# A two-layer encoder step: the first projection is computed from x without its reciprocal norm, and GpSimd multiplies the norm into each tile that it stores

## The chip, the cores and the metric

The kernel runs on one core of a Trainium2 chip. The metric is the device time of one execution, in microseconds (us). The three runs before the change took 2880.22, 2878.37 and 2882.38 us, with a median of 2880.22. A matmul runs on TensorE (PE in the profile; PEld is its weight load). DVE is VectorE, ACT is ScalarE, POOL is GpSimd, and SP is the queue that issues most transfers.

## The reference

Two layers work on 544 tokens (512 of a prompt and 32 of a second sequence) with 1024 channels. What matters here is the start of each layer:

```python
h = x * rsqrt(mean(x * x) + 1e-6) * g          # _rmsnorm, one factor per token, one gain per channel
a_q, a_k, a_v, a_f, b_q, b_k, b_v, c_in, gate_in = split(h @ w_in)   # 7944 columns wide
log_f = log_sigmoid(a_f + fox_forget_bias)
...                                            # three mixers: FoX attention, differential attention, RWKV-7
gates = sigmoid(gate_in)                       # 3 x 1024
y = sum(gates * proj) @ w_out
x = x + rmsnorm(y); x = x + rmsnorm(cross_attention(...)); x = x + rmsnorm(swiglu(...))
```

The reciprocal norm of a token is one number for all channels of that token. So it can be multiplied into the result of the projection instead of into its input: `(x * r * g) @ w = r * ((x * g) @ w)`.

## The kernel before

Everything is kept transposed: a tile has 128 channels as partitions and the 544 tokens as columns, so x is 8 such tiles (`xT`). A matmul takes 272 tokens (`HT`). To reach float32 accuracy with the fast matmul format, each operand is split into a high and a low part, and three products are summed (high x high, high x low, low x high): a tile of 128 output channels over 1024 input channels is 8 x 3 x 2 = 48 matmuls. Weights come in units of 128 output columns through a ring of 4 buffers that SP fills (`unit`, L447). DVE splits each unit into `WHI` and `WLO` (`split_unit`, L1867), of which there are two buffers; a unit's split starts when the tile that used that buffer is done.

The engines run five programs, written out by hand, that wait for each other by semaphores. Three barriers per layer (`phase_end`, L414) join PE, ACT, DVE and POOL; SP waits for the second one.

The start of a layer, before the change:
- layer 0 only: PE transposes the eight tiles of x (`setup`, L646, into three pairs of banks), ACT and DVE copy the two halves out.
- PE transposes the gain vectors (L777), ACT copies them to `VT`. ACT squares the 8 tiles of x (L1430); PE sums each over the channels (`norm_sums`, L692); ACT makes the reciprocal norm `RS` by Ln and Exp (`norm_rstd`, L1399).
- DVE splits weight units 0 and 1 (L1890, L1891). At the change of layers it does so after it has updated x (`postnorm`, L1849: hT * gain * RS, then xT += hT).
- After the first barrier, DVE makes h = x * gain * RS, its high and its low part, two tiles at a time (`prenorm_split`, L1834), and PE computes the tiles of units 0 and 1 together as the pairs arrive (`dense_first`, L748). From unit 2 on `dense_split` (L726) computes one tile after the other, all from the same `HH` and `hTR`.

The projection's results: 12 full tiles (`EST`, 4 buffers) and the forget gate's 8 rows in the first part; 26 tiles as 52 halves in fill between the attention's steps (`late`, `ESTL`, 4 buffers of a half); 24 gate tiles, of which 22 go out as 44 halves (`GST`), and the last two stay in the chip (`GS`, L1693: ACT applies the sigmoid as it copies them from PSUM). ACT (and DVE) copy a result from PSUM, POOL issues the store to DRAM, and SP loads it again where it is used. POOL computes nothing.

In front of the FFN the kernel already works in another manner: DVE updates x tile by tile, ACT makes the high part of x * gain as soon as a tile is updated, DVE the low part (`updated` and `low`, L2362 to L2370), `dense_first` starts with the first of them, the sums of squares are taken between its matmuls (`group_sums`, L673, and `sums_spread`, L685), and the reciprocal norm is multiplied in by DVE when it reads the results.

Of the kernel before, what the change touches and what calls it, by code (L numbers as in the profile page):

```python
# [8 lines left out]
F32 = mybir.dt.float32  # L9
# [3 lines left out]
ALU = mybir.AluOpType  # L13
# [41 lines left out]
X_SPLITS = 4 + 6 + 8  # L55
# [106 lines left out]
def build_program(nc, A, C_const, C_rope, O):  # L162
# [7 lines left out]
    with ExitStack() as ctx:  # L170
        def sb(name, shape, dt=F32):
            return ctx.enter_context(nc.sbuf_tensor(name, shape, dt))
# [7 lines left out]
        def sem(name):  # L180
            return ctx.enter_context(nc.semaphore(name))
# [16 lines left out]
        lam4 = sb("lam4", [P, 4, HEAD_DIM])  # L198
        lamp = sb("lamp", [P, 2, HEAD_DIM])
# [75 lines left out]
        FST = cv(3, 4)  # L275
        ESTL = carver(NU - KM * T - 4 * HT)(4, HT)
# [5 lines left out]
        for h in range(2):  # L282
# [65 lines left out]
        SUM_OF = (0, 6, 0, 6, 6, 6)  # L348
        SUMS_AT = (1, 2, 4, 5, 7, 8)
# [6 lines left out]
        ident_loaded, consts_loaded, x_loaded, x_put_act, setup_pe, consts_ready = (  # L356
            sem(n) for n in ("ident_loaded", "consts_loaded", "x_loaded", "x_put_act", "setup_pe", "consts_ready"))
# [283 lines left out]
        def _(pe):  # L641
# [3 lines left out]

            def setup():  # L646

                for a in range(KM):
                    if a % 4 == 0:
                        pe.wait_ge(*((x_loaded, 32) if a == 0 else (far_half, 16)))  # L650
                    if a >= 3:
                        pe.wait_ge(x_put_act, a - 2)
                        pe.wait_ge(x_updated, a - 2)
                    q = 2 + 2 * (a % 3)
                    for b in range(4):
# [29 lines left out]
            def sums_spread(l, k):  # L685

                pe.wait_ge(sums_put, l * 2 + k // 2)
# [85 lines left out]
            for l in range(DEPTH):  # L773

                pe.wait_ge(vec_loaded, (l + 1) * 16 * 19)
                pe.wait_ge(tile_freed_act, l * TILES + 4)
                tr(PS[:, 4, 0:NVEC], VR[0:NVEC, :], ident[0:NVEC, 0:NVEC]).then_inc(vec_turned, 1)  # L777
                norm_sums(l, 0)

                phase_end(pe, l, 0)  # L780
# [4 lines left out]
                dense_first(l, G_IN, 0, of_h_split, 0)  # L785
                for v in range(2, N_IN):
                    dense_split(l, G_IN + v, IN_PAIR[v], v, of_h_split, exact=(v == FORGET_AT), rot=IN_ROT[v])
# [442 lines left out]
                for n in range(N_BR):  # L1230
                    if n == 3:
                        pe.wait_ge(gt_evac, l * 48 + 50)
                    dense_split(l, G_BR + n, n % 4, V_BR + n, of_branch(n % 3), need=4 + 2 * n if n < 3 else None)
# [105 lines left out]
                dense_first(l, G_FFI, V_FFI, of_f, 10, sums=4)  # L1339
# [31 lines left out]
        def _(act):  # L1371
# [27 lines left out]
            def norm_rstd(l, k, to=RS):  # L1399

                if k in (2, 4):
                    act.wait_ge(sums_done, l * 8 + SUMS_AT[k] - 1)
# [3 lines left out]
                act.wait_ge(sums_done, l * 8 + SUMS_AT[k])  # L1406
                for h in range(2):
                    f(half(RS, h), PS[:, SUM_OF[k] + h, 0:HT], ACT.Ln, scale=1.0 / (D_MODEL * (GROUP if k in (2, 4) else 1)), bias=eps[:, 0:1])
# [15 lines left out]
            for l in range(DEPTH):  # L1424

                act.wait_ge(vec_turned, l + 1)
                copy(VT[:, 0:NVEC], PS[:, 4, 0:NVEC])
# [368 lines left out]
        def _(dve):  # L1796
# [12 lines left out]
            for a in range(KM):  # L1809
                dve.wait_ge(setup_pe, a + 1)  # L1810
                copy(xT[:, a, 2 * P:T], PS[:, 3 + 2 * (a % 3), 0:T - 2 * P]).then_inc(x_updated, 1)
            dve.wait_ge(ident_loaded, 16)
            dve.wait_ge(consts_loaded, 16)
            copy(identb[:, :], const("ident"))
            copy(mfoxb[:, :], const("mfox"))
            copy(mdiffb[:, :], const("mdiff"))
            dve.drain().then_inc(consts_ready, 1)

# [66 lines left out]

            for l in range(DEPTH):
# [3 lines left out]
                split_unit(l, 0)  # L1890
                split_unit(l, 1)  # L1891
                phase_end(dve, l, 0)
                prenorm_split(l, 0, "norm_mix_pre", HH)
# [3 lines left out]
                for v, j in enumerate(IN_ORDER):  # L1897
                    tile(l, G_IN + v)
                    split_unit(l, v + 2)
                    if j is None:  # L1900
                        for h in range(2):
                            ts(half(TZ[0:8, 0, :], h), PS[0:8, 6 + h, 0:HT], small[0:8, 20:21], None, ALU.add)
# [523 lines left out]
                postnorm(l, 5, "norm_ffn_post")  # L2426
# [9 lines left out]
        def _(pool):  # L2436
# [10 lines left out]
            for l in range(DEPTH):  # L2447

                for name, row in _v.items():
# [10 lines left out]
                    allow_slow_non_contiguous=True).then_inc(vec_loaded, 16)  # L2460
                dma(lam4[:, :, :].rearrange("p a b -> p (a b)"),
                    A["diff_lambda"][ds(l, 1)].rearrange("l a b -> l (a b)").to_broadcast([P, 256])) \
                    .then_inc(vec_loaded, 16)
                dma(PLF[:, :, :], A["cache_fox_logf"][ds(l, 1)].rearrange("l b (t p) h -> p (l b t) h", p=P)) \
                    .then_inc(plf_loaded, 16)
                wait(vec_loaded, (l + 1) * 16 * 19)
                wait(plf_loaded, (l + 1) * 16)
                phase_end(pool, l, 0)


# [5 lines left out]
                for v, j in enumerate(IN_ORDER):  # L2476
# [3 lines left out]
                    wait(tile_freed_dve, l * TILES + G_IN + v + 5)  # L2480
                    dma(proj_d[j * P:(j + 1) * P, :], EST[:, e % 4, :]).then_inc(est_stored[e % 4], 16)
# [19 lines left out]
                def late_store(q):  # L2501

                    wait(late_evac, l * 2 * N_LATE + q + 2)
                    r, h = (12 + LATE_ORDER[q // 2]) * P, q % 2
                    dma(proj_d[r:r + P, h * HT:(h + 1) * HT], ESTL[:, q % 4, :]).then_inc(late_stored[q % 4], 16)
                    if q >= 2:
                        late_kept(q - 2)
# [55 lines left out]
                def gate_store(q, it=0):  # L2563

                    for h in range(2):
                        wait(gt_evac, l * 48 + 2 * q + h + 3 + it * 16)
                        r = GATE_ORDER[q + it * 8] * P
                        dma(gate_d[r:r + P, h * HT:(h + 1) * HT], GST[:, q % 2, h, :]) \
# [39 lines left out]
                gate_kept(21)  # L2608
                wait(shift_stored, (l + 1) * 32)
# [5 lines left out]
                wait(sums_done, l * 8 + 2)  # L2615
# [51 lines left out]
```

## Time and profile before

| | |
|---|---|
| median of 3 runs | 2880.22 us |
| the profiled execution | 2874.14 us, span 2872.3 us |
| PE busy | 96% of the span |
| DVE / ACT / POOL busy | 56% / 26% / 9% |
| mean granted TensorE clock | 0.991 |

Busy means that an instruction of that engine ran. A line of a timeline gives start, duration, engine, line of the kernel, the operation, output and input, and, where the engine had been idle, for how long and who released it.

### The profile page before, as it was taken

How to read it: one execution, taken by the hardware profiler on the slowest of the kernel's cores; microseconds unless marked ns; L12 is line 12 of the kernel's file. 1: busy time of each engine (PE TensorE's matmuls, PEld its weight loads, DVE VectorE, ACT ScalarE, POOL GpSimd, SP SyncE). 2: the span in 40 equal slices, each digit the busy share in tenths (PEclk: the TensorE clock that was granted, in tenths of full speed). 3: DMA queues.
4: the chain of work that ended last, by engine and by line, in shares of the span. 5: the costliest groups of instructions: out<-in, count | busy, mean ns of one | idle time of the engine just before them, and what ended most of it. 6: DMA issues, size and time to landing. Idle time of an engine off the chain costs nothing.

```text
span 2872.3 us, 63037 instructions
## 1 busy us (share of the span) xinstructions
PE 2750.8 (96%) x26472; PEld 2571.1 (90%) x26472; DVE 1611.0 (56%) x2967; ACT 753.7 (26%) x1803; POOL 244.2 (9%) x423
## 2 busy tenths in 40 slices
PE   7999999999999989999989999999999998999998
PEld 6877889999999789999988778899999996999997
DVE  5444665666664266664374455556666533766633
ACT  1143343333332330000112433433223324200001
POOL 1221112000000100000001211110000000000000
PEclk9999999999999999999999999999999999999999
DMA  4453436222263133333234434452224532233231
GB/s 136 127 144 105 144 107 170 72 72 65 82 173 100 46 89 89 89 87 88 77 90 132 120 111 139 103 160 72 72 68 115 153 92 73 71 89 89 85 88 58
DMA packets 420762, 290.26 MB, mean 101 GB/s; under 512 B 38544, under 2 KB 386352, under 8 KB 420352
## 3 DMA queue, kind: packets, MB, share of 16 engines
q1 hardware_dynamic: 398496, 228.64, 28.7%
q0 software_dynamic: 21984, 57.59, 6.3%
q8 instruction: 210, 3.44, 0.5%
q14 instruction: 72, 0.59, 0.1%
HBM read 232.12 MB, written 54.07 MB: 100 GB/s over the span
## 4 chain that ended last, share of the span: by engine, by line
PE 80%; DVE 8%; ACT 3%; DVEq 3%; DMA 2%; issue 2%; ACTq 0%; SPq 0%
PE PS L744 35%; PE PS L813 10%; PE PS L1116 8%; PE PS L1049 7%; PE PS L722 4%; PE PS L1258 2%; DMA U<-gate_scratch 2%; ACT U L1373 1%; PE PS L859 1%; PE PS L1090 1%; ACT U L1376 1%; PE PS L895 1%; PE PS L763 1%; PE PS L974 1%; PE PS L1194 1%
## 5 line engine op out<-in xcount | busy, mean ns | idle before, releaser
L744 PE MATMUL PS<-U_r,WHI 128*128 128x272 f32 x2656 | 474.4, 289 | 12.5 <-DVEq L2285 9.0
L1376 ACT COPY U<-PS 128x272 f32<-128x272 f32 (+9 forms) x782 | 273.1, 373 | 728.3 <-PE PS L1116 139.8
L1865 DVE CAST WHI<-ring 128x1024 fp32r<-128x1024 f32 (+1 forms) x240 | 164.1, 684 | 473.3 <-PE PS L744 365.3
L744 PEld LDWEIGHTS PS<-U_r,WHI 128*128 128x128 f32 x2656 | 386.1, 188 | 18.1 <-DVEq L2285 13.2
L744 PE MATMUL PS<-brT_r,WHI 128*128 128x272 f32 x1728 | 357.3, 288 | 1.4 <-DVEq L1876 1.4
L744 PE MATMUL PS<-U_r,WLO 128*128 128x272 f32 x1696 | 350.0, 288 | 0.0
L744 PE MATMUL PS<-hT_r,WHI 128*128 128x272 f32 x1696 | 349.7, 288 | 0.0
L1875 DVE TENSOR_TENSOR WLO<-ring,WHI 128x1024 fp32r<-128x1024 f32 (+1 forms) x240 | 289.7, 1207 | 19.4 <-issue 1.3
L744 PE MATMUL PS<-brT_r,WLO 128*128 128x272 f32 x1344 | 278.2, 288 | 0.0
L744 PEld LDWEIGHTS PS<-brT_r,WHI 128*128 128x128 f32 x1728 | 271.5, 188 | 2.2 <-DVEq L1876 2.2
L813 PE MATMUL PS<-U_r,WHI 128*128 128x272 f32 x832 | 261.6, 314 | 12.2 <-ACT U L1376 12.0
L744 PEld LDWEIGHTS PS<-hT_r,WHI 128*128 128x128 f32 x1696 | 266.5, 189 | 0.0
L744 PEld LDWEIGHTS PS<-U_r,WLO 128*128 128x128 f32 x1696 | 265.6, 188 | 0.0
L813 PE MATMUL PS<-U_r,WLO 128*128 128x272 f32 x832 | 242.1, 291 | 0.0
L813 PE MATMUL PS<-hT_r,WHI 128*128 128x272 f32 x832 | 241.0, 290 | 0.0
L1049 PE MATMUL PS<-U_r,WHI 128*128 128x272 f32 x768 | 229.7, 299 | 2.8 <-DVEq L2080 2.4
L1049 PE MATMUL PS<-U_r,WLO 128*128 128x272 f32 x768 | 221.8, 289 | 0.0
L1049 PE MATMUL PS<-hT_r,WHI 128*128 128x272 f32 x768 | 220.9, 288 | 0.0
L1116 PE MATMUL PS<-U 64*64 64x64 f32 (+1 forms) x5184 | 213.2, 238 | 0.0
L744 PEld LDWEIGHTS PS<-brT_r,WLO 128*128 128x128 f32 x1344 | 209.8, 189 | 0.0
L1116 PEld LDWEIGHTS PS<-U 64*64 64x64 f32 x5184 | 207.2, 134 | 1.3
L813 PEld LDWEIGHTS PS<-U_r,WHI 128*128 128x128 f32 x832 | 158.7, 191 | 31.5 <-issue 15.0
(336 smaller groups left out, 4291.5 us busy)
## 6 DMA issues: line engine op xcount, KB each, us to landing
ring<-in_w_in_dram SPq DMA_DIRECT2D x126, 512.0 KB, 4.3
ring<-in_w_ffn_in_dram SPq DMA_DIRECT2D x88, 512.0 KB, 3.8
ring<-in_w_ffn_out_dram SPq DMA_DIRECT2D x32, 448.0 KB, 3.7
proj_scratch<-U POOLq DMA_DIRECT2D x104, 136.0 KB, 2.1
U<-proj_scratch SPq DMA_DIRECT2D x48, 272.0 KB, 4.2
ring<-in_w_branch_dram SPq DMA_DIRECT2D x48, 256.0 KB, 3.2
gate_scratch<-U POOLq DMA_DIRECT2D x88, 136.0 KB, 3.2
U<-gate_scratch SPq DMA_DIRECT2D x44, 272.0 KB, 2.9
```

Of the source, the lines that this page charges most:

```text
L722: ins = mm(PS[0:width, 2 * q + h, 0:HT], ring[:, n % RING, k, 0:width], rhs(k, h), start=(k == 0), stop=(k == kn - 1))
L744: ins = mm(PS[:, 2 * q + h, 0:HT], w, half(x, h), start=(first and k == 0 and n == 0), stop=(last and k == kn - 1 and n == len(terms) - 1))
L763: ins = mm(PS[:, 2 * j + h, 0:HT], w, half(x, h), start=(k == 0 and n == 0), stop=(k == KM - 1 and n == 2))
L813: ins = mm(PS[:, 7, 0:HT], w, half(x, h), start=(k == 0 and i == 0), stop=(k == 7 and i == 2))
L859: mm(PS[:, b, 0:n], q, FK[it % 2][0:66, h, 0:n], start=True, stop=False)
L895: ins = mm(PS[o, 6, i * P:(i + 1) * P], FVT[it % 2][:, h, t, :], pt[:, t * P:(t + 1) * P], start=(t == 0), stop=(t == i))
L1049: ins = mm(PS[:, 6 + h, 0:HT], w, half(x, h), start=(k == 0 and i == 0), stop=(k == 7 and i == 2))
L1116: ins = mm(PS[r, bank, cols], w_c[r], x_c[r], start=(n == 0), stop=(n == len(pairs) - 1))
L1258: ins = mm(PS[:, 2 + n % 4, u * P:(u + 1) * P], MNT[:, k, t * P:(t + 1) * P], ring[:, (U_MEM + 2 * s + u) % RING, k, :], start=(k == 0), s ...
L1376: return act.copy(out, in_)
L1865: copy(hi, src)
L1875: tt(lo, w, hi.bitcast(F32), ALU.subtract)
```

## The change

- **Projection input.** `HH` becomes the high part of x * gain, written by ACT (`high`), and `hTR` its low part, by DVE (`low_in`), one tile at a time, without the reciprocal norm. `dense_first` waits per tile (8 signals where there were 4) and has the sums of squares between its matmuls, in banks 4 and 5. The reciprocal norm goes to a buffer of its own, `RSI`, which lives until the gates.
- **Results.** POOL multiplies each tile or half by `RSI` before it issues the store (`scaled`): per layer 12 tiles, 52 late halves and 44 gate halves. The two gate tiles that stay in the chip are copied raw, multiplied by POOL, and then go through ACT's sigmoid in place. DVE multiplies the forget gate's 8 rows.
- **Order at the start.** In layer 0 DVE splits units 0 and 1 between its copies of x (after tiles 4 and 6), and PE transposes the vectors ahead of tile 6. At the change of layers DVE splits them as soon as the FFN's last tile is done, and then updates x and makes the low parts in one sequence (`update_and_split`).
- `diff_lambda` is loaded after the first barrier, into another place, and the first barrier is signalled but no longer waited for by PE, ACT and DVE.

The diff, cut to its core:

```diff
-                pe.wait_ge(vec_loaded, (l + 1) * 16 * 19)
-                pe.wait_ge(tile_freed_act, l * TILES + 4)
-                tr(PS[:, 4, 0:NVEC], VR[0:NVEC, :], ident[0:NVEC, 0:NVEC]).then_inc(vec_turned, 1)
-                norm_sums(l, 0)
-                phase_end(pe, l, 0)
+                if l > 0:
+                    pe.wait_ge(tile_freed_act, l * TILES + 4)
+                    vectors(l, 4)
+                pe.drain().then_inc(bar, 1)
-                dense_first(l, G_IN, 0, of_h_split, 0)
+                dense_first(l, G_IN, 0, of_h_split, 0, sums=0)
+                sums_spread(l, 0)
...
+                def high(a):
+                    act.wait_ge(x_updated, l * 24 + a + 1)
+                    f(HH[:, a, :], xT[:, a, :], ACT.Copy, scale=vec("norm_mix_pre", a)).then_inc(h_ready, 1)
-                for a in range(KM):
+                for a in range(0, KM, 2):
+                    high(a)
+                    high(a + 1)
                     norm_square(l, 0, a)
-                norm_rstd(l, 0)
-                phase_end(act, l, 0)
+                    norm_square(l, 0, a + 1)
+                norm_rstd(l, 0, RSI[:, :])
...
                 for q in (22, 23):
                     for h in range(2):
                         act.wait_ge(gt_done, l * 48 + 2 * q + h + 1)
-                        f(half(GS[:, q - 22, :], h), PS[:, 6 + h, 0:HT], ACT.Sigmoid).then_inc(gt_evac, 1)
+                        copy(half(GS[:, q - 22, :], h), PS[:, 6 + h, 0:HT]).then_inc(gt_evac, 1)
+                    gate_cast(q + 2)
+                for q in (22, 23):
+                    act.wait_ge(gs_scaled, l * 2 + q - 21)
+                    f(GS[:, q - 22, :], GS[:, q - 22, :], ACT.Sigmoid)
                     act.drain().then_inc(gs_ready, 1)
-                    gate_cast(q + 2)
                 phase_end(act, l, 1)
...
+            def low_in(l, b):
+                dve.wait_ge(h_ready, l * 24 + b + 1)
+                stt(hTR[:, b, :], xT[:, b, :], vec("norm_mix_pre", b), HH[:, b, :].bitcast(F32), ALU.mult, ALU.subtract) \
+                    .then_inc(x_split, 1)
+            def update_and_split(l):
+                dve.wait_ge(rstd_ready, l * 6 + 6)
+                scale(0); scale(1); dve.drain(); add(0); add(1)      # scale: hT * gain * RS; add: xT += hT
+                for b in range(2, KM, 2):
+                    scale(b); scale(b + 1); dve.drain()
+                    low_in(l + 1, b - 2); low_in(l + 1, b - 1)
+                    add(b); add(b + 1)
+                low_in(l + 1, KM - 2); low_in(l + 1, KM - 1)
+            for a in range(KM):
+                dve.wait_ge(setup_pe, a + 1)
+                copy(xT[:, a, 2 * P:T], PS[:, 3 + 2 * (a % 3), 0:T - 2 * P]).then_inc(x_updated, 1)
+                if a == 4:
+                    split_unit(0, 0)
+                if a == 6:
+                    split_unit(0, 1)
...
-                postnorm(l, 5, "norm_ffn_post")
+                if l == DEPTH - 1:
+                    postnorm(l, 5, "norm_ffn_post")
+                else:
+                    tile(l, G_FFO + N_FFO - 1)
+                    split_unit(l + 1, 0)
+                    split_unit(l + 1, 1)
+                    dve.drain().then_inc(bar, 1)
+                    update_and_split(l)
...
+                def scaled(t, h=None):                                # POOL
+                    by = RSI[:, :] if h is None else half(RSI, h)
+                    pool.tensor_tensor(t, t, by, ALU.mult)
+                    pool.drain()
+                    scaled(EST[:, e % 4, :])                          # ahead of the store, and so for ESTL and GST
                     dma(proj_d[j * P:(j + 1) * P, :], EST[:, e % 4, :]).then_inc(est_stored[e % 4], 16)
```

## Rows read from the trace of the kernel before

**Rows 1.** The page: busy time, share of the span and instructions of each engine.
```profile
PE 2750.8 (96%) x26472; PEld 2571.1 (90%) x26472; DVE 1611.0 (56%) x2967; ACT 753.7 (26%) x1803; POOL 244.2 (9%) x423
```
**Rows 2.** The chain that ended last, its longest pieces: start us, us, what.
```profile
34.79 13.20 PE PS L763 x84
50.49 14.31 PE PS L744 x112
...
1043.88 385.41 PE PS L744 x3072
1468.35 14.29 PE PS L744 x112
```
**Rows 3.** Timeline at the change of layers.
```profile
1429.12 2.91 PE L703 MATMUL PS<-brT,ones 128*128 128x272 f32 x12
...
1433.72 1.48 DVE L1858 SCALAR_TENSOR_TENSOR hT<-hT,small,U 128x544 f32<-128x544 f32 x2 [13.15 <-ACTq L1411]
```
**Rows 4.** Timeline of the start of the FFN in layer 0.
```profile
1034.83 1.12 PE L680 MATMUL PS<-U,ones 128*32 128x272 f32 x16
...
1041.80 0.69 DVE L1865 CAST WHI<-ring 128x1024 fp32r<-128x1024 f32 x1 [3.04 <-PE PS L763]
```
**Rows 5.** Timeline of the first 30 us.
```profile
10.99 0.52 POOL L2459 DMA_DIRECT2D small<-in_fox_forget_bias_dram  x1
...
14.22 0.46 DVE L1811 COPY xT<-PS 128x288 f32<-128x288 f32 x1 [0.83 <-PE PS L657]
...
15.40 1.11 PE L656 MATMUL PS<-CB,U 128*128 128x128 f32 x4
...
19.49 0.69 DVE L1865 CAST WHI<-ring 128x1024 fp32r<-128x1024 f32 x1
...
21.60 0.69 DVE L1865 CAST WHI<-ring 128x1024 fp32r<-128x1024 f32 x1
```
**Rows 6.** Transfers issued at 3.3 to 3.9 and 4.4 to 12 us: KB, us to landing.
```profile
ring<-in_w_in_dram SPq DMA_DIRECT2D x1, 512.0 KB, 11.8
...
small<-in_fox_forget_bias_dram POOLq DMA_DIRECT2D x1, 0.0 KB, 5.1
```
**Rows 7.** Groups of instructions: shapes, count | busy us, mean ns | idle before.
```profile
L2369 DVE SCALAR_TENSOR_TENSOR hT_r<-xT,VT,brT_r 128x544 fp32r<-128x544 f32 x16 | 12.5, 779 | 0.2
...
L1855 DVE TENSOR_TENSOR xT<-xT,hT 128x544 f32<-128x544 f32 x32 | 21.8, 722 | 1.2
...
L1373 ACT ACTIVATE brT_r<-xT,VT 128x544 fp32r<-128x544 f32 x16 | 12.0, 749 | 17.0 <-DVE xT L2365 17.0
```
**Rows 8.** Stretches: length, busy us of PE, PEld, DVE, ACT, POOL, granted clock, DMA.
```profile
29.30:33.00 3.70, 0.00 (x0) 0.00 (x0) 1.94 (x3) 1.47 (x3) 0.00 (x0) 1.00 0.00 0
34.79:40.00 5.21, 5.21 (x23) 5.21 (x24) 4.95 (x7) 0.00 (x0) 0.00 (x0) 0.50 0.01 3
```
**Rows 9.** Timeline from the last gate tile into the branch projection, layer 0.
```profile
759.47 0.62 ACT L1376 CAST WHI<-ring 128x512 fp32r<-128x512 f32 x1
...
760.14 0.69 DVE L2103 TENSOR_TENSOR WLO<-ring,WHI 128x512 fp32r<-128x512 f32 x1 [1.14 <-ACTq L1581]
...
766.78 0.52 PE L744 MATMUL PS<-U_r,WHI 128*128 128x272 f32 x2 [1.23 <-DVEq L2285]
```
**Rows 10.** Timeline of ACT among the first gate tiles.
```profile
475.26 0.39 ACT L1376 COPY U<-PS 128x272 f32<-128x272 f32 x1 [2.70 <-POOLq L2561]
```
**Rows 11.** POOL's groups of instructions: count | busy us, mean ns | idle before.
```profile
L2505 POOL DMA_DIRECT2D proj_scratch<-U x104 | 57.3, 551 | 451.3 <-ACT U L1376 400.8 <-DVEq L2080 41.9 <-issue 8.6
L2568 POOL DMA_DIRECT2D gate_scratch<-U x88 | 48.1, 548 | 206.1 <-ACT U L1376 200.0 <-issue 6.2
```
**Rows 12.** Timeline of the preparation of one RWKV recurrence.
```profile
550.28 0.87 ACT L1376 COPY U<-PS 128x272 f32<-128x272 f32 x2
...
550.38 1.36 DVE L2134 TENSOR_TENSOR U<-U 128x545 f32<-128x545 f32 x2
...
554.44 1.24 PE L1090 MATMUL PS<-U,CB 128*128 128x288 f32 x4 [0.40 <-DVE U L2157]
```

More of the change, by code:

```diff
@@ L54 @@
 SPLITS = V_FFO + 8 * len(FFO_SPLIT)
-X_SPLITS = 4 + 6 + 8
+X_SPLITS = 8 + 6 + 8
 def unit_of(v):
@@ L644, in _, with vectors @@
             pe.wait_ge(ident_loaded, 16)
+            def vectors(l, bank):
+                pe.wait_ge(vec_loaded, l * 16 * 19 + 16 * 18)
+                tr(PS[:, bank, 0:NVEC], VR[0:NVEC, :], ident[0:NVEC, 0:NVEC]).then_inc(vec_turned, 1)
             def setup():
@@ L654, in setup @@
                     q = 2 + 2 * (a % 3)
+                    if a == 6:
+                        vectors(0, 0)
                     for b in range(4):
@@ L1337, in of_f @@
                     return HF[:, k, :], hTR[:, k, :]
-                dense_first(l, G_FFI, V_FFI, of_f, 10, sums=4)
+                dense_first(l, G_FFI, V_FFI, of_f, 14, sums=4)
                 sums_spread(l, 4)
@@ L1405, in norm_rstd @@
                     act.drain().then_inc(sums_put, 1)
-                act.wait_ge(sums_done, l * 8 + SUMS_AT[k])
+                act.wait_ge(sums_done, l * SUMS + SUMS_AT[k])
                 for h in range(2):
-                    f(half(RS, h), PS[:, SUM_OF[k] + h, 0:HT], ACT.Ln, scale=1.0 / (D_MODEL * (GROUP if k in (2, 4) else 1)), bias=eps[:, 0:1])
+                    f(half(RS, h), PS[:, SUM_OF[k] + h, 0:HT], ACT.Ln, scale=1.0 / (D_MODEL * (GROUP if k in (0, 2, 4) else 1)), bias=eps[:, 0:1])
                 act.drain()
@@ L1808, in _ @@
             dve.sem_inc(df_evac, 1)
[L1809 to L1817, printed above, removed]
             def add_square(l, k, a):
@@ L1884, in split_x, with scale, add @@
                     tt(lo_a, src_a, hi_a.bitcast(F32), ALU.subtract).then_inc(x_split, 1)
+            def low_in(l, b):
[3 more added lines that the diff above has]
+            def update_and_split(l):
+                def scale(b):
+                    stt(hT[:, b, :], hT[:, b, :], ffn_gain(b), RS, ALU.mult, ALU.mult)
+                def add(b):
+                    tt(xT[:, b, :], xT[:, b, :], hT[:, b, :], ALU.add).then_inc(x_updated, 1)
+                dve.wait_ge(rstd_ready, l * 6 + 6)
+                scale(0)
+                scale(1)
+                dve.drain()
+                add(0)
+                add(1)
+                for b in range(2, KM, 2):
+                    scale(b)
+                    scale(b + 1)
+                    dve.drain()
+                    low_in(l + 1, b - 2)
+                    low_in(l + 1, b - 1)
+                    add(b)
+                    add(b + 1)
+                low_in(l + 1, KM - 2)
+                low_in(l + 1, KM - 1)
+            for a in range(KM):
[3 more added lines that the diff above has]
+                    split_unit(0, 0)
+                if a == 6:
+                    split_unit(0, 1)
+            dve.drain().then_inc(bar, 1)
+            for b in range(KM):
+                low_in(0, b)
+            dve.wait_ge(ident_loaded, 16)
+            dve.wait_ge(consts_loaded, 16)
+            copy(identb[:, :], const("ident"))
+            copy(mfoxb[:, :], const("mfox"))
+            copy(mdiffb[:, :], const("mdiff"))
             for l in range(DEPTH):
@@ L1900, in _ @@
                     if j is None:
+                        dve.wait_ge(rstd_ready, l * 6 + 1)
                         for h in range(2):
-                            ts(half(TZ[0:8, 0, :], h), PS[0:8, 6 + h, 0:HT], small[0:8, 20:21], None, ALU.add)
+                            tt(half(TZ[0:8, 0, :], h), PS[0:8, 6 + h, 0:HT], half(RSI[0:8, :], h), ALU.mult)
+                        dve.drain()
+                        ts(TZ[0:8, 0, :], TZ[0:8, 0, :], small[0:8, 20:21], None, ALU.add)
                         dve.drain().then_inc(lf_step, 1)
@@ L2460, in _ @@
                     allow_slow_non_contiguous=True).then_inc(vec_loaded, 16)
+                dma(PLF[:, :, :], A["cache_fox_logf"][ds(l, 1)].rearrange("l b (t p) h -> p (l b t) h", p=P)) \
+                    .then_inc(plf_loaded, 16)
+                wait(vec_loaded, l * 16 * 19 + 16 * 18)
+                wait(plf_loaded, (l + 1) * 16)
+                phase_end(pool, l, 0)
                 dma(lam4[:, :, :].rearrange("p a b -> p (a b)"),
@@ L2608, in _ @@
                 gate_kept(21)
+                for q in (22, 23):
+                    wait(gt_evac, l * 48 + 2 * q + 4)
+                    pool.tensor_tensor(GS[:, q - 22, :], GS[:, q - 22, :], RSI[:, :], ALU.mult)
+                    pool.drain().then_inc(gs_scaled, 1)
                 wait(shift_stored, (l + 1) * 32)
@@ L2614, in _ @@
                 dma(mtok[:, :, :], A["mem_prompt"].rearrange("b (t p) d -> p (b t) d", p=P)).then_inc(mem_loaded, 16)
-                wait(sums_done, l * 8 + 2)
+                wait(sums_done, l * SUMS + 3)
                 for t, name in ((CKT, "cache_mem_k"), (CVT, "cache_mem_v")):
```

40 lines of the change are left out of this document (20 added, 20 removed).

## The prediction, made before the changed kernel was run

> **What bounds the kernel now.** I read the busy shares first: PE works for 96% of the span and POOL for 9% [rows 1]. With such a PE, time can only be won where PE is idle, or slow, and only lost where something new makes it wait. So next I read the chain that ended last for the places where it leaves PE. At the start of layer 0 the first matmul of the projection comes at 34.79 us and the third tile (unit 2) at 50.49; at the start of layer 1 the third tile comes at 1468.35 [rows 2], 39 us after the FFN's last tile, which ends where the sums of its output begin, at 1429.12 [rows 3]. The timelines of these two places say what fills the gap: squares, sums, reciprocal norm, then h, its high part and its low part, and only then a matmul. Elsewhere the chain is matmuls back to back, 385.41 us for 3072 of them in the FFN, 0.1255 us each [rows 2]. The changed start has a model in this kernel, the start of the FFN [rows 4]. Then I looked at where DVE leads PE, because that is where a busier POOL could hurt.
>
> **The start of layer 0.** The new order removes the squares, sums and norm from in front of the first matmul.
> - PE's transposes of the vectors now stand ahead of tile 6 and wait for the bias vector: issued at 10.99, 5.1 us to landing, so 16.1 instead of 15.40 [rows 5, 6]; with some 0.4 us for the transposition itself, tiles 6 and 7 come 1.1 us later. They end at about 19.2.
> - DVE copies tile 4 until 14.7 [rows 5]. Unit 0 was issued at 3.4 and lands 11.8 us later [rows 6], 15.2. A split takes 21.60 - 19.49 = 2.1 us [rows 5], so 17.3; the copies of tiles 5 and 6 (0.46 each), 18.4; the split of unit 1, 20.5; the copy of tile 7 and a drain, 21.1; the first low part, 0.78 us [rows 7], 21.9. ACT's high part of tile 0 is ready by 20.9, so it does not count. The first matmul comes at 22.1.
> - From there PE is the slower one: a tile of x gives it 12 matmuls, 1.5 us, while ACT and DVE deliver one in less (ACT a high part at 0.75 [rows 7] and a square that is no longer, DVE 0.78). So 8 x 12 x 0.1255 = 12.05 us, and two groups of sums at 1.1 [rows 4]: 36.3. Tile 0 is ready 6 matmuls before the end, 35.6; then DVE splits unit 2, and PE has it 2.15 us later, as in the FFN (cast from 1041.80, next tile at 1043.88 [rows 2, 4]). The sums' spread and ACT's copy lie inside that. The third tile starts at 37.8 where it started at 50.49: **12.7 us won**.
> - The clock. Before, PE was idle from 29.3 and was still granted 1.00 until 33.0 [rows 8]; when it began again at 34.79 it had 0.50 (the 1.2 GHz level) for 5.2 us [rows 8]. The new gap, 19.2 to 22.1, is shorter than the 3.7 us that the row shows without a fall, so I take the full clock. If it falls, half of 5.2 us, 2.6, comes back.
>
> **The change of layers.** DVE now waits for the FFN's last tile, 1429.2 [rows 3], splits two units, 2 x 2.1 = 4.2 us, and so is at the update at 1433.6; the norm releases it at 1433.72 as before [rows 3]. The splits cost nothing there. Then a scale and a low part are 0.78 each and an add 0.72 [rows 7]; with the overlap seen in the trace a pair of tiles takes 4.35 us. First low part: two scales, two adds, two scales, one low: 1438.9. The others arrive at 1439.7, 1443.3, 1444.0, 1447.6, 1448.3, 1450.4 and 1451.1. ACT's high parts follow each add by 0.75 and are ready before DVE asks. PE starts at 1439.0 after 7 us of idleness, so at the low clock; 5.2 us of it lose 2.6. It is then busy almost without a gap: 1439.0 + 12.05 + 2.2 + 2.6 + 0.2 = 1456.0, tile 0 at 1455.3, the third tile at 1457.5 where it was 1468.35: **10.9 us won**. Both starts: 23.6.
>
> **The end of the gates.** The second barrier holds SP's loads for the branch projection, and the branch tiles that wait for them start with PE idle (1.23 us at 766.78 [rows 9]). So a later barrier goes straight to the end. Before, ACT's last cast ended at 760.1 and DVE's subtract at 760.83 [rows 9]. Now POOL multiplies the last gate tile (copied when ACT's cast begins at 759.47; two halves' time, 1.4 us by the estimate below) and ACT does a sigmoid of 544 columns after it, 0.75 us by the nearest row [rows 7], until 761.7. Cost 0.9 per layer, 1.8 in all, between 0 (a multiply under 0.6) and 4.
>
> **POOL's multiplications.** No row shows POOL computing, so I bound one. Below: a half of 272 columns takes 0.39 us on ACT from PSUM [rows 10]. Above I know no limit in this trace. I take 0.72, DVE's time for two inputs of twice the length [rows 7]. Per layer there are 96 halves and 14 tiles. On POOL's own time they are nothing: its stores are idle 451 and 206 us while they wait for ACT [rows 11]. They delay the release of a staging buffer by one or two multiplies. That is tightest among the first gates, where ACT's copy at 475.26 already waited 2.70 us for POOL [rows 10]; two multiplies and a store issue (0.55 [rows 11]) put it at about 477.2, and PE wants that bank one half (24 matmuls, 3.0 us) after it left it at 475.2. It holds by 1 us: 0, up to 2 us a layer if a multiply takes over 1.2.
>
> What can cost is DVE. In the preparation of each of the 8 recurrences PE waits for DVE (0.40 us at 554.44 [rows 12]), so every delay of DVE there is a delay of the kernel; and POOL multiplies beside it, for instance behind the copies that begin at 550.28 while DVE subtracts SBUF tiles from 550.38 [rows 12]. Four multiplies lie beside that path and four behind it, where DVE has more than 1 us to spare. Whether they hold each other up no row shows: 0 us if not, 4 x 0.72 = 2.9 and some 0.4 behind it if each holds DVE for its full length. Between ends so far apart I take a good third of it, 1.1 per recurrence, **9 us**, because a multiply often begins beside a DVE instruction that reads PSUM, or in a wait. In the attention stages PE has matmuls to fill with; 0.6 in all, up to 5.
>
> The Trainium skill (SBUF — State Buffer, Who interferes with whom) speaks against this change: a DVE instruction with two SBUF inputs, or a copy in its two-port mode, and a GpSimd instruction that reads SBUF exclude each other, and the later one blocks for the whole of the other. By that rule the holding is whole and the sum is near the second rival's; no run here shows it yet. The GPSIMD Engine Reference (Elementwise, side by side) gives 4497 ns against 2293 for a two-input add of 2048 elements; an estimate from that page for 272 is 0.6 us, a little under my 0.72.
>
> **Sum.** -12.7 - 10.9 + 1.8 + 9 + 0.6 = -12.2 us. The profiled execution took 2874.14 (span 2872.3), so 2861.9; the median of the runs shown is 6.1 above it, and the same change puts it at 2868.
>
> **Rivals.**
> 1. Nothing holds DVE: the multiplies fall into gaps. -23.6 + 1.8 = -21.8, median 2858. For: POOL's idle time, and DVE busy only 56%. Against: DVE has instructions back to back in the preparation [rows 12].
> 2. Each multiply beside the path holds DVE for 0.72: 8 x 3.3 = 26.4 instead of 9. -23.6 + 1.8 + 26.4 + 0.6 = +5.2, median 2885: nothing is left of the gain.
> 3. Slower: the same holding, with a multiply of more than 0.9 us. At 1.2 us it is 8 x (4.8 + 1.5) = 50, less 21.8, +28, median 2908; it is slower than before from 2.7 us of holding per recurrence on. For: GpSimd may be slow with two inputs. Against: nothing in the trace, it has no such row.
> 4. The starts win less: the clock falls at 22 us (2.6), or the units land late. That moves any of the above by up to 4 us and has no case of its own.
>
> **Chances.** The forecast (0.4 to 1.8 us held per recurrence, 2862 to 2875) 0.40; rival 1, 0.27; rival 2 (2875 to 2889) 0.23; rival 3 0.10. For this kernel 0.2%, 5.8 us, is about what a measurement tells from no change. Faster than 2874.4: 0.27 and nearly all of the forecast's 0.40, less a little for rival 4, 0.63. Within 2874.4 and 2886: 0.22. Slower: 0.15. The range from 2854 (rival 1 with starts that win 4 us more) to 2885 leaves out about 2 in 10.
>
> **What would show it.** Third tiles at 37.8 and near 1445 to 1457 (layer 1 also shifted by what layer 0 won); PE at clock 1.00 from 22 us; the group sums between the matmuls. On POOL a multiply of 128x272 with a mean near 0.7 us. In the preparation the DVE rows of two SBUF inputs (0.72 to 0.76 us before) longer in the mean, and PE's wait for DVE above 0.40: 1.5 there is my forecast, 0.4 is rival 1, 3.3 is rival 2. The forecast is wrong if the starts win under 20 us, or if DVE's rows are unchanged, or if PE waits for POOL's buffers among the gates.

## The result and the profile after

The changed kernel is slower: 2919.69 us (median of 4 runs) against 2879.3 us, a ratio of 1.0143 with a 95% interval of 1.0129 to 1.0157. The forecast was 2868 us. Its profiled execution took 2914.4 us of span (2872.3 before). Both starts are won, nearly as forecast; about three times as much is lost later, above all among the first gates.

The page, busy time of each engine, answers to [rows 1]. PE does the same work in a longer span, and POOL nearly doubles.

```profile
PE 2752.3 (94%) x26480; PEld 2571.6 (88%) x26480; DVE 1660.3 (57%) x2953; ACT 765.7 (26%) x1827; POOL 460.5 (16%) x643
```

The chain that ended last, longest pieces (start us, us, what), answers to [rows 2]. Long pieces called issue are new: in them POOL stood, and nothing that the profile shows was waited for.

```profile
21.91 9.50 PE PS L772 x60
...
67.73 42.20 PE PS L753 x336
...
436.87 14.79 issue
453.05 4.76 issue
...
515.48 29.78 PE PS L1126 x792
...
1066.54 384.24 PE PS L753 x3072
1460.55 10.30 PE PS L772 x60
...
1873.85 13.03 issue
1888.28 4.76 issue
```

From the same pieces in both traces I take the length of each stretch and subtract that of the kernel before (us; the marks are the 336 matmuls of the projection, the load of the differential cache, the first and the last recurrence's burst of 792 matmuls, the 150 matmuls of the output projection, and the FFN; the stretch to the 336 matmuls of layer 1 is taken from the FFN before it):

| stretch | layer 0 | layer 1 |
|---|---|---|
| start, to the 336 matmuls | -9.9 | -11.5 |
| FoX attention, to the differential cache | +4.7 | +0.6 |
| differential attention and first gates, to the first burst | +22.0 | +22.0 |
| three pitches of the recurrences | +5.7 | +5.7 |
| end of the gates and branch projection | +0.1 | +3.0 |
| to the FFN | +0.1 | -0.8 |

Two stretches of 22.0 us are more than the whole loss of 42.1. POOL's timeline at the first gates of layer 0 (start, us, engine, line, operation; in brackets the idle time before) shows what happens there:

```profile
433.81 1.94 POOL L2628 DMA_DIRECT2D out_dram<-proj_scratch  x2 [2.25 <-DMA proj_scratch<-U]
435.76 1.11 POOL L2536 TENSOR_TENSOR U<-U,RSI 128x272 f32<-128x272 f32 x1
451.66 0.60 POOL L2641 DMA_DIRECT2D gate_scratch<-U  x1 [14.79 <-issue]
452.28 0.77 POOL L2536 TENSOR_TENSOR U<-U,RSI 128x272 f32<-128x272 f32 x1
457.82 0.58 POOL L2641 DMA_DIRECT2D gate_scratch<-U  x1 [4.77 <-issue]
458.40 0.77 POOL L2652 DMA_DIRECT2D proj_scratch<-U  x1
459.19 0.77 POOL L2536 TENSOR_TENSOR U<-U,RSI 128x272 f32<-128x272 f32 x1
463.14 0.60 POOL L2641 DMA_DIRECT2D gate_scratch<-U  x1 [3.19 <-issue]
```

A multiplication takes 0.77 us here, the first one 1.11. Between it and its store stands a drain (`scaled`, L2536 and the line after), an instruction at which POOL stops for its own earlier work; it is there so that the store reads the finished product. It is this drain that lasts 14.79, 4.77 and 3.19 us. The last transfers that POOL had issued before the first two of them, with KB and us to landing:

```profile
out_dram<-proj_scratch POOLq DMA_DIRECT2D x1, 7.0 KB, 16.2
...
gate_scratch<-U POOLq DMA_DIRECT2D x1, 136.0 KB, 5.6
```

The first (the second of the two single-element transfers of L2628) was issued at 434.8 and landed at 451.0; the drain let go at 451.66. The second was issued at 451.66 and landed at 457.3; the next drain let go at 457.82. So in both windows the drain ended just behind the landing of POOL's own transfer, and the staging buffers came back late; the experiments test whether that is the cause. The waits (engine, line, waited for: us in total, times, longest) carry it to PE, in an order of POOL, ACT, PE:

```profile
POOL gate_scratch L2641 <- issue: 163.0, 88, 14.8
...
ACT U L1386 <- POOLq L2633: 99.3, 16, 20.1
PE PS L1059 <- ACT U L1386: 37.3, 12, 13.9
...
PE PS L1100 <- DVE U L2214: 9.3, 6, 1.6
```

Before, ACT had waited for POOL at this semaphore 18.9 us in all, 4.8 at most (the copy of [rows 10] 2.70), and PE had not waited for these copies at all:

```profile
ACT U L1376 <- POOLq L2561: 18.9, 6, 4.8
```

The row of L1100 is the holding of DVE: PE waits for DVE 1.6 us there, and had waited 0.40 in [rows 12]. Two stretches of the windows view (length, busy us of PE, PEld, DVE, ACT, POOL, granted clock, DMA) show the wait and what follows it: the clock has fallen to 0.50, the 1.2 GHz level, and the matmuls that follow start 0.227 us apart, where they are 0.126 apart from 473 us on.

```profile
454.00:467.80 13.80, 0.00 (x0) 0.00 (x0) 0.91 (x1) 0.45 (x2) 3.97 (x6) 0.57 0.70 224
468.00:472.00 4.00, 4.00 (x18) 4.00 (x19) 0.99 (x1) 2.33 (x7) 1.51 (x2) 0.50 0.62 244
```

### The profile page after: what moved, and what is told of

Its sections match the earlier page's. It is cut to its first block, busy times and chain, and to the rows that moved or that the text cites. A ratio compares the mean times of both kernels' runs of the same rounds, so it can differ in the third digit from the quotient of the medians.

```text
span 2914.4 us, 63493 instructions
## 1 busy us (share of the span) xinstructions
PE 2752.3 (94%) x26480; PEld 2571.6 (88%) x26480; DVE 1660.3 (57%) x2953; ACT 765.7 (26%) x1827; POOL 460.5 (16%) x643
## 4 chain that ended last, share of the span: by engine, by line
PE 74%; DVE 9%; issue 6%; DVEq 3%; DMA 3%; ACT 3%; POOLq 1%; POOL 1%; ACTq 0%; SPq 0%
PE PS L753 34%; PE PS L823 9%; PE PS L1126 8%; PE PS L731 4%; PE PS L1059 3%; PE PS L1268 2%; DMA U<-gate_scratch 2%; PE PS L869 1%; PE PS L772 1%; ACT U L1383 1%; PE PS L1100 1%; DVE WLO L1886 1%; ACT U L1386 1%; POOLq L2537 1%; PE PS L1204 1%
## 5 line engine op out<-in xcount | busy, mean ns | idle before, releaser
L1386 ACT COPY U<-PS 128x272 f32<-128x272 f32 (+10 forms) x794 | 275.7, 372 | 761.9 <-PE PS L1126 140.0
L753 PEld LDWEIGHTS PS<-U_r,WHI 128*128 128x128 f32 x2656 | 385.7, 189 | 18.0 <-DVEq L2342 13.3
L1886 DVE TENSOR_TENSOR WLO<-ring,WHI 128x1024 fp32r<-128x1024 f32 (+1 forms) x240 | 303.9, 1266 | 19.3 <-issue 1.3
L2536 POOL TENSOR_TENSOR U<-U,RSI 128x272 f32<-128x272 f32 (+1 forms) x216 | 201.0, 931 | 486.5 <-ACT U L1386 385.5
```

The costliest lines, as they stand in the source:

```text
L753: ins = mm(PS[:, 2 * q + h, 0:HT], w, half(x, h), start=(first and k == 0 and n == 0), stop=(last and k == kn - 1 and n == len(terms) - 1))
L1386: return act.copy(out, in_)
L1886: tt(lo, w, hi.bitcast(F32), ALU.subtract)
L2536: pool.tensor_tensor(t, t, by, ALU.mult)
```

## The experiments

All ratios are to the kernel before, run on the same chip. Theory D: a drain of POOL also waits until POOL's transfers under way have landed. Theory M: the multiplication itself is what costs. They share the holding of DVE (theory H). A pitch is the time from the start of one recurrence's burst to that of the next.

**a1_sem.** POOL waits for its multiplication by a semaphore.

```diff
-                    pool.tensor_tensor(t, t, by, ALU.mult)
-                    pool.drain()
+                    pool.tensor_tensor(t, t, by, ALU.mult).then_inc(mul_done, 1)
+                    pool.wait_ge(mul_done, n)     # n counts the multiplications
```

> POOL multiplies as in the changed kernel, but waits for its own multiplication by a semaphore and not by a drain. In the changed kernel POOL stands up to 14.79 us between a multiplication and its store, and the stretch from the first gates to the first recurrence's burst lost 22.0 us in each layer. Theory D (the drain also waits until POOL's transfers under way have landed, so a staging buffer is released late and PE starves): that stall goes, the stretch loses at most 3, and the time is about 2919.7 - 2 x 20 = 2880 (2868 to 2888); the recurrences still come 1 to 2 us later each than before. Theory M (the multiplication itself is what delays the release and DVE): nothing changes, 2915 to 2920.

Measured 2900.85 us, 1.0085 (1.0068 to 1.0101). From a multiplication to its store it is 0.30 us now:

```profile
438.57 0.60 POOL L2645 DMA_DIRECT2D gate_scratch<-U  x1 [0.30 <-POOL U L2539]
```

The stretch of the first gates loses 6.6 and 5.2 us instead of 22.0: theory D, not M. But the whole is 21 us above the 2880 expected: the three pitches lose 11.3 and 9.8 us (5.7 before this edit), and the end of the gates 8.0 and 7.5. Both were new, and b1 and b3 follow them. The stretches are those of the profiled execution, which took 2909.41 us, 8.6 above the median, so they overstate a little; b1, with the same code up to the end of the gates, loses 1.9 and 2.9 us at the first gates and 9.9 and 9.9 in the pitches.

**a2_drain_only** and **a3_neither.** The drains without the multiplications, and neither.

```diff
                 def scaled(t, h=None):
-                    pool.tensor_tensor(t, t, by, ALU.mult)
                     pool.drain()                  # a3_neither: this line too is left out
```

> The drains stay, the multiplications by the reciprocal norm are left out (the projections and gates lack the norm). Theory D: the stretch of the first gates still loses about 20 us a layer; only what the multiplications held of DVE (some 1.9 us per recurrence, and part of 4.7 in the first layer's attention) comes back: 2895 to 2905. Theory M: all of it comes back, 2857 to 2862.

> Neither drain nor multiplication (the projections and gates lack the norm). Both theories: what the starts alone are worth. From the traces the starts won 9.9 and 11.4 us; less the later end of the gates, 2857 to 2862. If it comes out above 2868, something else in the change costs too.

a2 measured 2895.48 us, 1.0064 (1.0049 to 1.0079): the first gates lose 20.6 and 18.8 us though POOL computes nothing there, while the pitches lose 0.4 and 0.0. Its first gate store:

```profile
445.35 0.56 POOL L2640 DMA_DIRECT2D gate_scratch<-U  x1 [16.32 <-issue]
```

a3 measured 2863.63 us, 0.9958 (0.9944 to 0.9973), a little above the 2857 to 2862 expected: the starts alone win, and the first gates and the pitches lose under 1 us. What a3 lost was at the end of the gates, 6.4 and 6.6 us. Its chain there:

```profile
748.83 0.02 POOLq L2683
748.84 0.08 issue
748.92 6.83 POOLq L418
```

L418 is the drain ahead of the second barrier. POOL's last transfer had been issued at 737.03 and landed 2.0 us later, so nothing was in flight, and still it took 6.83 us. It was the first drain since the start of the layer.

**a4_shift_later.** The two transfers of single elements go behind the first recurrence.

```diff
-                for src, to in ((SEQ - 1, p_shift), (T - 1, s_shift)):   # ahead of gate_store(0)
...
                         wait(rp_done, g + 1)
+                        if it == 0 and p == 0:    # the same two transfers here
```

> As the changed kernel, but the two transfers of single elements (the shift states, 12.6 us to landing) are issued by POOL after the first recurrence instead of ahead of the first gate store. Theory D: the longest wait between a multiplication and its store falls from 14.8 to 3 to 5 us at the first gates, the stretch loses 8 instead of 22 in each layer, and a shorter wait may come up after the first recurrence, where PE does not need the buffer: 2885 to 2897. Theory M: 2915 to 2920.

Measured 2919.53 us, 1.0153 (1.0138 to 1.0168). The first gates lose 9.4 and 11.7 us, near the 8 expected, but the pitches now lose 18.2 and 17.7: the same drain stands at the new place, for 13.5 us, and PE does need the buffer there. My 2885 to 2897 was wrong in that. The wait travels with the transfers, as D says; nothing is saved.

**e1_one_drain.** The kernel before, with one drain a layer.

```diff
                         proj_d[R_RW:R_RW + RWKV_IN, src:src + 1], ...).then_inc(shift_stored, 16)
+                pool.drain()
```

> The kernel before with one drain of POOL a layer and nothing else: right behind the issue of the two transfers of single elements, ahead of the first gate store. Theory D (a drain waits until the transfers under way have landed): POOL stands there for 14 to 17 us and the first gate store is issued at some 453 instead of 437.80. The store would have landed only behind those transfers anyway, at some 456, so PE pays only for the difference and for the stores that are bunched up behind it, 3 to 6 us a layer: 2882 to 2889. Rival (a drain waits for POOL's own computing alone, and it was the multiplication that stood there): POOL stands under 1 us, no change, 2876.

Measured 2889.77 us, 1.0048 (1.0035 to 1.0061). POOL's timeline, with no multiplication anywhere:

```profile
437.27 1.94 POOL L2556 DMA_DIRECT2D out_dram<-proj_scratch  x2 [2.04 <-DMA proj_scratch<-U]
456.01 1.09 POOL L2570 DMA_DIRECT2D gate_scratch<-U  x2 [16.80 <-issue]
```

One drain stands 16.80 us and costs 6.4 and 7.6 us a layer, a little over the 3 to 6 expected. This shows a long stand of POOL at a drain without the rest of the change. It costs far less than the changed kernel's 22.0; there every store behind the first had a drain of its own (4.77, 3.19 us), which would explain the difference, though no run separates it.

**b1_early_drain.** On a1: the drain of the second barrier is taken before the last two multiplications.

```diff
                 gate_kept(21)
+                wait(shift_stored, (l + 1) * 32)
+                pool.drain()
                 for q in (22, 23):
...
-                phase_end(pool, l, 1)
+                wait(gs_scaled, (l + 1) * 2)      # then signal and wait for the barrier, without a drain
```

> a1_sem with one more edit: POOL's drain ahead of the second barrier, which took 8.44 us after the last multiplication there, is taken before the last two gate tiles are multiplied (after the last store has landed), and the barrier is signalled behind the multiplications alone. Theory E (a drain that comes first after some hundred transfers takes 7 to 8 us though nothing is in flight, and a1_sem exposed it at the end of the gates; in the kernel before, it lay beside the last two gate tiles): 6 us a layer come back, 2900.9 - 12 = 2889 (2885 to 2893), and from the last recurrence to the output projection it is 143 to 145 us again instead of 151. Rival: what waits there is something else than the drain, and the time stays at 2901.

Measured 2884.16 us, 1.0026 (1.0016 to 1.0036), 17 us under a1 by the ratios and a little better than the 2885 to 2893 expected. The end of the gates loses 2.1 and 0.4 us instead of 8.0 and 7.5.

**b3_no_gate_mul, b2_double, c3_one_input.** On b1: no multiplication of the gates; every multiplication twice; a multiplication by a constant, with one input.

```diff
-                    pool.tensor_tensor(t, t, by, ALU.mult)
+                    pool.tensor_scalar(t, t, 1.0, None, ALU.mult)        # c3_one_input
```

> b1_early_drain without the multiplications of the gates (they lack the norm); the first tiles and the late halves are still multiplied by POOL. Theory H (a multiplication on POOL holds DVE, and DVE leads PE in the preparation of the recurrences): the recurrences' pitch is 67.5 us again as before (71.3 in a1_sem), the first gates lose nothing, and what is left of the cost is the first layer's attention, some 5 us: 2855 to 2864. Rival (POOL's slower release of the staging buffers costs the recurrences, not the holding): the same pitch, but DVE's instructions with two SBUF inputs in the preparation show the same means in both kernels.

> b1_early_drain with each multiplication of a stored tile or half done twice (so it is multiplied by the square of the norm). Theory H: the holding doubles. In the preparation DVE's subtraction of 545 columns goes from 1.07 us towards 1.4 in the mean, the pitch of the recurrences from 71.3 to 74 or more (3.8 us over the kernel before become 7 to 9), and the whole is 2889 + 8 x 4 + 8 = 2929 (2915 to 2945). Rival (no holding, the multiplications fall into gaps of DVE): the pitch moves by less than 1 us.

> b1_early_drain with POOL multiplying each stored tile or half by the constant 1.0 (tensor_scalar, one input) instead of by the reciprocal norm (tensor_tensor, two inputs); the projections and gates lack the norm. Theory H1 (what holds DVE is the second input that POOL reads): the pitch falls to 67.5 and DVE's rows to 0.72 to 0.76 us, 2855 to 2866. Theory H2 (any instruction of POOL that reads SBUF holds DVE): the pitch stays above 70 if the instruction is as long as a multiplication of two inputs, 2880 to 2890, and lies between if it is shorter.

| kernel | us | ratio (interval) | three pitches, layers 0 and 1 |
|---|---|---|---|
| b1_early_drain | 2884.16 | 1.0026 (1.0016 to 1.0036) | +9.9, +9.9 |
| b3_no_gate_mul | 2863.03 | 0.9948 (0.9931 to 0.9965) | +0.4, +0.0 |
| b2_double | 2925.21 | 1.0169 (1.0145 to 1.0193) | +19.7, +18.2 |
| c3_one_input | 2864.30 | 0.9957 (0.9944 to 0.9970) | +2.4, +2.2 |

b3 leaves the norm out of the gates, c3 out of all stored projections and gates, and b2 multiplies by its square. The cost per pitch is about 0, 3.3 and 6.3 us for none, one and two multiplications: a straight line. DVE's groups of the preparation (busy us, mean ns) in b1:

```profile
L2192 DVE TENSOR_TENSOR U<-U 128x545 f32<-128x545 f32 x24 | 23.3, 1001 | 0.6
L2229 DVE TENSOR_TENSOR U<-U 128x576 f32<-128x576 f32 x8 | 10.6, 1328 | 0.0
```

in b3:

```profile
L2192 DVE TENSOR_TENSOR U<-U 128x545 f32<-128x545 f32 x24 | 16.7, 725 | 0.6
...
L2229 DVE TENSOR_TENSOR U<-U 128x576 f32<-128x576 f32 x8 | 6.0, 750 | 0.0
```

and in c3, with POOL's instruction:

```profile
L2539 POOL TENSOR_SCALAR U<-U 128x272 f32<-128x272 f32 x192 | 194.0, 1010 | 443.9 <-ACT U L1387 412.0 <-DVEq L2138 30.5
...
L2192 DVE TENSOR_TENSOR U<-U 128x545 f32<-128x545 f32 x24 | 18.1, 784 | 0.6
L2229 DVE TENSOR_TENSOR U<-U 128x576 f32<-128x576 f32 x8 | 7.8, 980 | 0.0
```

So a multiplication of two inputs holds DVE's instructions of two inputs. With one input it holds them less in all, though it is longer (1010 ns against 882), but not row by row. Added up over DVE's rows of the preparation (L2192 to L2237, all eight recurrences) the busy time above b3's is 28 us in b1, 52 in b2 and 10 in c3; one of these rows, L2232, is even longer in c3 than in b1 (1172 ns against 887). c3 thus lies between its two theories, nearer to the first. b1's pitch costs more than the holding: PE waits 1.84 us there, and its windows behind that wait are

```profile
552.00:556.00 4.00, 4.00 (x21) 3.95 (x20) 3.69 (x7) 1.85 (x3) 0.62 (x1) 0.57 0.00 0
556.00:560.00 4.00, 4.00 (x31) 3.44 (x30) 3.92 (x5) 1.33 (x2) 2.68 (x4) 1.00 0.58 166
```

By an estimate from the row, the clock at 0.57 costs some 1.7 us of the first 4 (4.00 x 0.43). In the changed kernel the wait was 1.6 us, the clock stayed at 1.00, and a pitch cost 1.9.

**b4_early_split.** The kernel before with the first weights split ahead of the update of x.

```diff
+                tile(l, G_FFO + N_FFO - 1)
+                split_unit(l + 1, 0)
+                split_unit(l + 1, 1)
                 postnorm(l, 5, "norm_ffn_post")
```

> The kernel before with one part of the change alone: at the change of layers DVE splits the first two weight units ahead of the update of x. Theory S (these splits lay beside ACT's squares, PE's sums and the norm, and the start was won by leaving these out of the path): within 0.1% of before, the third tile of layer 1 at 1468 plus or minus 1. Rival (the 4.2 us of splits were on the path, since the norm of the update releases DVE only at 1433.72): 4 us faster, third tile at 1464.

Measured 2873.76 us, 0.9989 (0.9980 to 0.9998): some 0.1%, 0.2% at most. The third tile of layer 1 comes 424.66 us behind the FFN's first matmul, 424.47 before, where the rival wanted 4 us less. So at the change of layers the early split alone wins nothing. What did win there is the deferred norm together with the work tile by tile; no run separates these two, and none the order at the start of layer 0.

**d1_late_mul** and **d2_drain_in_burst.** On b1: the gates go out raw, and POOL multiplies them where PE does not wait for DVE; d2 adds a drain there.

```diff
-                        scaled(GST[:, q % 2, h, :], h)         # kept for tile 21 alone
...
+                # behind the third gate store of each preparation, beside the burst:
+                # load a stored tile into GST, multiply it, store it again; five or six tiles
+                gate_rework(range(at, at + (6 if at == 15 else 5)))
+                pool.drain()                                   # d2_drain_in_burst alone
```

> b1_early_drain, but POOL stores the gate tiles raw among the first gates and in the preparation of the recurrences, and multiplies them later: in each recurrence's burst, where POOL stood idle for some 35 us, it loads five or six stored tiles back into its two staging buffers, multiplies and stores them again (21 tiles of 128x544 a layer at some 1.4 us; the 22nd is multiplied as it is stored). The reference's computation is kept. Theory H (what cost was that POOL's multiplications hold DVE's two-input instructions of the preparation, which lead PE; in the burst DVE reads PSUM and PE does not wait for it): the pitch is 67.5 to 68 us again, the burst stays at 29.8, the stretch of the first gates loses nothing, and the time is that of b3_no_gate_mul, 2863, plus at most 5: 2861 to 2870, 0.3 to 0.5% under the kernel before. Rival (the multiplications hold DVE wherever they stand): the burst grows by 1 to 3 us each, 2872 to 2888. Second rival: the reloads do not fit into the burst and the last gate tile of a recurrence waits for its staging buffer: the pitch is over 69.

> d1_late_mul with POOL draining also at the end of the multiplications in each recurrence's burst, where it has 9 to 11 us left. Theory E (a drain's own time grows with the transfers issued since the one before it): the drain ahead of the last two multiplications, which in d1_late_mul held them until 757.08 although the first gate tile had been copied at 750.98, becomes short, the two multiplications follow their copies, and the second barrier comes 1.6 us earlier in each layer: 2869.2 - 3 = 2866 (2863 to 2868). Rival (that drain takes 8 us whatever precedes it): 2869, and the second barrier where it was.

d1 measured 2869.24 us, 0.9973 (0.9963 to 0.9983), and d2 2865.01 us, 0.9960 (0.9946 to 0.9974), and neither leaves anything out: d2 is faster than the kernel before by 12 us and, by the two ratios, than the changed one by 53. The pitches lose 1.6 and 0.3 us in d2, and DVE's subtraction of 545 columns is back at 724 ns. The row of that subtraction, and POOL, in d2, first in a burst, then at the end of the gates:

```profile
L2192 DVE TENSOR_TENSOR U<-U 128x545 f32<-128x545 f32 x24 | 16.7, 724 | 0.6
...
503.46 1.33 POOL L2540 TENSOR_TENSOR U<-U,RSI 128x544 f32<-128x544 f32 x1 [3.39 <-DMA U<-gate_scratch]
505.09 0.60 POOL L2652 DMA_DIRECT2D gate_scratch<-U  x1 [0.30 <-POOL U L2540]
505.72 1.35 POOL L2540 TENSOR_TENSOR U<-U,RSI 128x544 f32<-128x544 f32 x1
...
751.44 1.62 POOL L2715 TENSOR_TENSOR U<-U,RSI 128x544 f32<-128x544 f32 x1 [4.32 <-ACT U L1387]
757.40 1.65 POOL L2715 TENSOR_TENSOR U<-U,RSI 128x544 f32<-128x544 f32 x1 [4.33 <-ACT U L1387]
```

In d1 the two last multiplications stood until 757.08, though the first tile's copy had ended at 750.98 and the last store had landed at some 748.2; here each follows ACT's copy. That is theory E: a drain that comes after another is short. (In d1 757.08 is also 0.07 us behind the copy of the second tile, so its drain may have ended a little earlier.) The two ratios overlap: that d2 is the faster kernel is not shown.

## Why the prediction was wrong, point by point

- **The start of layer 0** (12.7 us forecast). The first matmul came at 21.91 (22.1) and the group sums stood between the matmuls, but the third tile came at 39.79, not 37.8: 10.7 won. PE's timeline says why (a row is two matmuls):

```profile
21.91 0.79 PE L772 MATMUL PS<-U_r,WHI 128*128 128x272 f32 x2 [3.00 <-DVE hT_r L1900]
...
23.41 0.65 PE L772 MATMUL PS<-U_r,WHI 128*128 128x272 f32 x2
23.86 0.66 PE L772 MATMUL PS<-hT_r,WHI 128*128 128x272 f32 x2
...
28.99 0.41 PE L772 MATMUL PS<-U_r,WHI 128*128 128x272 f32 x2
29.24 0.41 PE L772 MATMUL PS<-hT_r,WHI 128*128 128x272 f32 x2
...
39.79 0.52 PE L753 MATMUL PS<-U_r,WHI 128*128 128x272 f32 x2 [0.45 <-DVEq L1887]
```

  Until 25.98 the first 18 matmuls came 0.45 us a pair, later ones 0.25: the pace that the matmuls above had at 0.50 (0.227 apart), though the record of the granted clock reads 1.00 there. That is 1.8 of the 2.0 us. Rival 4 had named it at 2.6; the reading that a gap of this length leaves the full clock was wrong.
- **The change of layers** (10.9). From the sums of the FFN's output to the third tile it was 39.06 us and is 28.44 (1450.79 to 1479.23): 10.6 won, with the clock at 0.50 for the first 4.5 us (5.2 taken). Right.
- **The end of the gates** (1.8). ACT's copy of the last gate half to SP's first load took 2.03 us in layer 0 and takes 3.00 now: 0.97, forecast 0.9. The stretch lost 0.1 and 3.0 us. Right in the sum, by luck in part: the sum has no term for the drain of the barrier itself, which stood in the path for 6.83 us in a3 and 8.44 in a1. The changed kernel was spared it: ACT's last sigmoid started 0.09 us behind the last multiplication (783.49 and 783.40) and SP's first load followed at 784.28. That agrees with theory E, since the drains of `scaled` had gone just before.
- **Holding of DVE** (9). Mechanism right, size short: 1.9 a pitch, 15 us over eight recurrences. PE's wait at the first one compared was 1.6, forecast 1.5. The mean of POOL's multiplication was 0.86 us for 272 columns, forecast 0.72. The prediction's estimate from the Trainium skill (GPSIMD Engine Reference, Elementwise — side-by-side), 0.6, was lower still. In b1 it is 3.3 a pitch, 26 us, the second rival's number, of which part is the clock's. By the Trainium skill's rule (SBUF — State Buffer, Who interferes with whom), a DVE instruction with two SBUF inputs contends with a GpSimd instruction that reads SBUF. The traces agree for two inputs (724 to 1001 ns). For one input, which also reads SBUF, the holding is about a third (10 us of 28, c3 against b1). In FoX attention it was 4.7 and 0.6 us, where I had taken 0.3 a layer; a3 there shows -0.6 and -2.7.
- **The step that failed** is "On POOL's own time they are nothing ... It holds by 1 us: 0, up to 2 us a layer if a multiply takes over 1.2". A multiplication took 0.77 us there, and the cost was 22.0 us a layer less about 1.9 for the first recurrence, 20 us, 40 in all. I had priced `scaled` as its multiplication. The drain in it, which the diff shows, has no term in the sum; a2 and e1 show it lasting 16.3 and 16.8 us with no computing there. [rows 11] gave 200.0 of POOL's 206.1 us of idle time as a wait for ACT, but that held for a kernel with no drain ahead of a store. For the multiplications alone the step held: without the drains, in b1, the first gates lose 1.9 and 2.9 us, no more than its first recurrence's 3.3, though the 2.70 us of [rows 10] was not the longest wait (4.8).

The sum by what was measured: -21.4 (starts), +5.4 (FoX), +44.0 (to the first burst, the first recurrence's holding in it), +11.3 (pitches), +3.2 and -0.8 at the end, 41.7 of the 42.1 us between the spans. None of my rivals held the drain. The last sign of being wrong, "if PE waits for POOL's buffers among the gates", named the place and the wait, but the sum had no cost or cause for it. Rival 3 had the sign right (+28), but by multiplications of 1.2 us, and they took 0.86.

What stays open: what a drain does in the 7 to 8 us with nothing in flight. a3, b1, d1 and d2 show that it is long after many transfers and short soon after another drain; no run varied the number alone. In e1, too, the second transfer landed some 3 us before the drain let go, so not all of its 16.80 us is the wait for the landing.

## What to carry to other kernels

Price a helper by each of its instructions, the waits too: on POOL, which issues transfers here, a drain was also a wait for them, and a semaphore on the one instruction was not. Before work goes to an idle engine, look at which engine the bound one waits for at that moment: multiplying the gates cost 21 us beside DVE's preparation (b1 less b3) and some 3 us beside the burst (d2 less b3 by their ratios, within the noise). Where a slack is 1 us, say what would eat it, and look for every wait in the new code that could.

## What the runs showed of the hardware

- POOL's drain ends 0.5 to 0.7 us after its last transfer in flight lands where it is one of many drains (451.0 and 451.66; 457.3 and 457.82). A wait on the instruction's own semaphore took 0.30 us.
- The first drain after a layer's transfers took 6.83 us with none in flight.
- The two transfers of single elements (7.0 KB each) took 9.1 and 16.2 us to land. In a1 the first gate stores, issued at 438.57 and 440.29 behind them, took 15.5 and 16.52 us.
- POOL's multiplication of two inputs: 0.77 us alone and 0.86 to 0.88 us in the mean for 128x272, 1.33 to 1.35 us for 128x544 beside the burst; DVE takes 0.72 for the latter [rows 7]. With one input its mean was 1.01 us for 128x272, longer than with two.
- DVE's subtraction of 128x545 beside POOL's multiplications: 977 ns in the mean in the changed kernel and 1001 in b1, 724 without them.
